# Weight ring of a transformer stack: host-ordered weights, and two expert units per transfer

## The chip, the cores and the metric

The kernel runs on one core of a Trainium2 chip. The metric is device time in microseconds (us) from start to end of one execution; lower is better.

## The reference, cut to what matters

Two blocks follow each other on 256 tokens of width 1024, all in float32. Each layer of the first block has a mixer (windowed attention in layer 0, a gated linear recurrence in layer 1) and then a mixture of experts; these two expert layers hold nearly all the weights (16 experts of 12.6 MB each, per layer). The second block has two mixers ("even" and "odd") with modulation vectors computed from `ada_w`.

```python
def expert_choice_moe(x, w_router, w_gate_up, w_down):
    aff = softmax(x @ w_router)                       # 256 x 16
    gates, idx = top_k(swapaxes(aff, 1, 2), 32)       # 32 tokens for each expert
    xs = x[bi, idx]
    g, u = split(einsum('becd,edf->becf', xs, w_gate_up), 2, axis=-1)    # 1024 x 2048 each
    out = einsum('becf,efd->becd', silu(g) * u, w_down) * gates[..., None]   # 1024 x 1024 each
    return zeros_like(x).at[bi, idx].add(out)
```

## The kernel before, in words

**The ring.** All large weights pass through a ring of eight places in the on-chip memory, `B.slot[0]` to `B.slot[7]`, of one *unit* each: 16 KB a partition, 2 MB over 128 partitions. A ninth place, the spare (number 8), lies elsewhere. An expert has four gate-up units (`gu<layer>_<expert>_<k>`) and two down units (`down<layer>_<expert>_<k>`). Other units hold the attention weights (`qkv`, `o`), the modulation weights (`ada`), the weights of the recurrence (`lru`, `rgate`, `igate`), three context units that lie between the expert units of layer 0 (`ctx_kv`, `ctx_v_lr`, `ctx_ckr`) and the weights of the even and odd mixers.

**The order.** `units()` (L240) writes out the order in which units are fetched, with the place of each and the unit that was there before. `FIRST_UNITS` (L86) fixes by hand the places of the first units of each expert layer, while modulation units still pass through. After them every unit takes the next place of the rotation (L284 to L286): eight places in layer 0, nine with the spare in layer 1. Thus a unit goes to the place that was filled longest ago.

**The fetches.** `loads()` (L511) is the program of the SyncE queue (SPq in the profile). It goes through the list in order; before each transfer it waits until the previous occupant of the place is free (L525), then issues one transfer (L536), and nothing later can pass it. The last expert of a layer fetches each down unit in four pieces (L530). A unit is set free by the matmul that reads it last: L1408 for gate-up units (after 16 matmuls of L1406), L1438 for down units (after 32 matmuls of L1436), L1475 for the last down units.

**The experts on TensorE.** `experts_tensor()` (L1340) takes the experts one by one: it waits for each gate-up unit, multiplies (L1406), hands over to ScalarE and VectorE for the activation, turns it (L1418), waits for each down unit and multiplies (L1436). Before the first expert of a layer it routes and gathers tokens (L1514, L1515), and once more between the up and the down products of the first expert. In layer 0 it also calls a side program after every second unit, which computes the context part of the even mixer from the three context units. For the last expert, two additions on TensorE (L1399) stand before each of the gate-up units 2 and 3, and `last_outs_tensor()` (L1460) multiplies the down pieces as they arrive (L1472) and adds the outcome to the tokens (L1481).

**Row lengths.** `unit_parts()` (L553) gives source and destination of each transfer. A gate-up unit reads 16 KB in one run per partition, a down unit two runs of 8 KB, most of the others eight runs of 2 KB. The two `o` units are fetched by eight transfers of 64 partitions each.

**Rounding.** For the mixers' products ScalarE (L364) writes a rounded copy of a unit into the place of `<name>_hi`, and VectorE (L380) the rest into the unit's own place. The even mixer begins with `even_narrow`, the odd mixer uses the gate blocks `ada14` and `ada15`.

Of the kernel before, what the change touches and what calls it, by code (L numbers as in the profile page):

```python
# [14 lines left out]
P = 128  # L15
D = 1024
S = 256
H = S // P
T = D // P
DEPTH = 2  # L20
# [106 lines left out]
    return out  # L127


class Signals:  # L130


# [104 lines left out]
    pass  # L237


def units():  # L240

    order, occupant, state = [], {}, {"slots": list(range(SLOTS)), "at": 0}
# [30 lines left out]
    for layer in range(DEPTH):  # L273
        experts = expert_units(layer)
        occupant[SPARE] = "lru1" if layer else None
        ring = []
        for c, i in FIRST_UNITS[layer]:
            slot = SPARE if i == SPARE else turn[i]
            if c is None:
                put(next(experts), slot)  # L280
                ring.append(slot)
            else:
                put(f"ada{layer}{c}", slot)
        state["slots"], state["at"] = ring if layer else [slot for slot in ring if slot != SPARE], 0  # L284
        for name in experts:
            put(name)  # L286
        if layer == 0:
            first = [state["slots"][(state["at"] + i) % SLOTS] for i in range(SLOTS)]
# [26 lines left out]
class Program:  # L315
# [195 lines left out]
    def loads(self):  # L511
        sig, sp, d, B = self.sig, self.sp, self.d, self.B
        sp.dma_start(B.ident, d["k_ident"]).then_inc(*sig.tell("ident_loaded", ("ident",), by=16))
        x_rows = d["x"].rearrange("o (h p) d -> p (o h) d", p=P)
        for half in range(H):
            sp.dma_start(B.x[:, half, :], x_rows[:, half, :]).then_inc(*sig.tell(f"x{half}_loaded", ("x", "input", half), by=16))
        for name, slot, before in B.units:
            if name.endswith("_hi") or name == "decay_room":
                continue
            if before is not None:  # L520
                sp.wait_ge(*sig.after("free", before))
            if name.startswith("down") and name.split("_")[1] == str(NE - 1):
                (dst, src), = self.unit_parts(name, B.slot[slot])
                for i in range(PACK):
                    sp.dma_start(dst[:, i], src[:, i]).then_inc(*sig.tell(f"last{name[-1]}{i}_loaded", ("arrived", name, i), by=16))  # L525
                continue
            if name == "qkv2":
                (dst, src), = self.unit_parts(name, B.slot[slot])
                for i in range(4):
                    pair = slice(2 * i, 2 * i + 2)  # L530
                    sp.dma_start(dst[:, pair], src[:, pair]).then_inc(*sig.tell(f"first{i}_loaded", ("arrived", name, i), by=16))
# [12 lines left out]
        sp.wait_ge(*sig.after("stored"))  # L544

    def late_rows(self):
# [3 lines left out]
        for dst, key in ((B.gain, "ln_mix_g"), (B.bias, "ln_mix_b")):  # L550
            sp.dma_start(dst, d[key][0].partition_broadcast(P)).then_inc(*sig.tell("first_rows", ("rows", "attention"), by=16))

    def unit_parts(self, name, slot):  # L553
        d = self.d
        tiles = lambda w, c0, c: w.rearrange("(p t) n -> p t n", t=T)[:, :, c0:c0 + c]
        view = lambda c: slot[:, 0:T * c].rearrange("p (t c) -> p t c", t=T)
        outs = {"lru_out": ("lru_w_out", "lru_out"), "even_out": ("even_w_out_2", "even_out"),
                "odd_out": ("odd_w_out_2", "odd_out")}
        if name[:-1] == "o":
            rows = lambda m, i: d["attn_w_o"][0][(2 * m + i) * GROUP * HD:(2 * m + i + 1) * GROUP * HD, int(name[-1]) * 512:][:, 0:512]  # L560
            return [(view(512)[64 * i:64 * i + 64, m * GROUP:(m + 1) * GROUP, :], rows(m, i).rearrange("(g d) n -> d g n", g=GROUP))
                    for m in range(2) for i in range(2)]
        if name[:-1] in outs:
            return [(view(512), d[outs[name[:-1]][0]][0].rearrange("(t p) n -> p t n", p=P)[:, :, int(name[-1]) * 512:][:, :, 0:512])]
        if name.startswith("qkv"):
            return [(view(512), tiles(d["attn_w_qkv"][0], int(name[3:]) * 512, 512))]
        if name.startswith("ada"):
            return [(view(512), tiles(d["ada_w_2"][int(name[3])], int(name[4]) * 512, 512))]
        if name.startswith("gu"):
            layer, e, k = (int(i) for i in name[2:].split("_"))  # L570
            rows = d["moe_w_gate_up"][layer][e].rearrange("(p t) n -> p t n", t=T)
            return [(slot.rearrange("p (t n) -> p t n", t=2), rows[:, 2 * k:2 * k + 2, :])]
        if name.startswith("down"):
            layer, e, k = (int(i) for i in name[4:].split("_"))
            if e == NE - 1:
                rows = d["moe_w_down"][layer][e].rearrange("(j c s) n -> c j s n", j=PACK, s=2)
                return [(slot.rearrange("p (j s n) -> p j s n", j=PACK, s=2), rows[:, :, :, k * 512:(k + 1) * 512])]
            rows = d["moe_w_down"][layer][e].rearrange("(j c s) n -> c j (s n)", j=PACK, s=2)
            return [(slot.rearrange("p (j n) -> p j n", j=2), rows[:, 2 * k:2 * k + 2, :])]
        if name.startswith("ctx"):  # L580
            _, c0, c = next(w for w in CTX_W.values() if w[0] == name)
            return [(view(c), tiles(d["even_w_in_2"][0], c0, c))]
        if name in ("lru0", "lru1", "lru2", "lru3"):
            return [(view(512), tiles(d["lru_w_in"][0], int(name[3]) * 512, 512))]
        if name in ("rgate", "igate"):
            src = d[f"lru_w_{name}"][0].rearrange("z n (c p) f -> p (z n c) f", p=P)
            return [(slot.rearrange("p (b f) -> p b f", f=LBW), src)]
        if name == "mla":
            return [(slot[:, 0:NU].rearrange("p (k n) -> p k n", k=KQ), d["mla_w_uq_2"][0].rearrange("(k p) n -> p k n", p=P)),
                    (slot[:, UNIT - MH * (MN + MV):UNIT], d["mla_w_ukv_2"][0])]  # L590
        if name.startswith("even"):
            ranges = dict(EVEN_W)[name[5:]]
            c, at, parts = sum(n for _, n in ranges), 0, []
            for c0, n in ranges:
                parts.append((view(c)[:, :, at:at + n], tiles(d["even_w_in_2"][0], c0, n)))
                at += n
            return parts
        return [(view(512), tiles(d["odd_w_in_2"][0], dict(ODD_W)[name[4:]], 512))]

    def feature_pair(self, stage, name, w, cols, h, bank, width=P):  # L600

# [2528 lines left out]
def buffers(nc, ctx):  # L3130
# [16 lines left out]
    B.slot, B.slot_r = (list(s) for s in zip(*[M.take_both(f"weight_ring{i}", UNIT) for i in range(SLOTS)]))  # L3147
# [144 lines left out]
def build(nc, dram, out):  # L3292
    with ExitStack() as ctx:
# [3 lines left out]
            Program(nc, sig, buf, dram, out, rows_dram, counting).build()  # L3297


_INS = ['x', 'attn_w_qkv', 'attn_w_o', 'attn_sink', 'lru_w_in', 'lru_conv_w', 'lru_conv_b', 'lru_w_rgate', 'lru_b_rgate',  # L3300
        'lru_w_igate', 'lru_b_igate', 'lru_lambda', 'lru_w_out', 'moe_w_router', 'moe_w_gate_up', 'moe_w_down', 'ln_mix_g',
        'ln_mix_b', 'ln_ffn_g', 'ln_ffn_b', 'c_2', 'ctx_2', 'c_ctx_2', 'ada_w_2', 'ada_b_2', 'post_ln_g_2', 'post_ln_b_2',
        'even_w_in_2', 'gla_w2_2', 'gla_b_2', 'gla_norm_g_2', 'mla_q_norm_g_2', 'mla_w_uq_2', 'mla_kv_norm_g_2', 'mla_w_ukv_2',
        'even_w_out_2', 'odd_w_in_2', 'sgu_w_2', 'sgu_b_2', 'odd_w_out_2']


# [13 lines left out]
```

## Time and profile before

| | |
|---|---|
| median of 3 runs | 1452.27 us (1452.17 to 1452.87) |
| the profiled execution | 1454.88 us, its span 1453.5 us |
| TensorE busy, mean granted clock | 1119.1 us (77%), 0.893 |
| VectorE, ScalarE, GpSimd busy | 469.0, 319.6, 91.8 us |
| SyncE's transfers (queue q1) | 492.78 MB, 83.9% of 16 engines' span |
| chain that ended last | transfers 51%, TensorE 33%, VectorE 7%, ScalarE 5% |

The span runs from the first to the last instruction; 1.4 us of the profiled execution lie around it. The layers of experts take about 118 to 590 us (layer 0) and 706 to 1165 us (layer 1). In the views of stretches the DMA column is the mean busy share of the 16 DMA engines, GB/s what they moved, and PEclk the granted clock of TensorE, 1.00 for the full 2.4 GHz and 0.50 for 1.2 GHz.

### The profile page before, as it was taken

The numbers are of one execution on the slowest core, as the hardware profiler recorded it, in microseconds if no ns is written. First come the engines' busy times: TensorE is split into PE (matmuls) and PEld (weight loads), VectorE is DVE, ScalarE is ACT, GpSimd is POOL, SyncE is SP. The second block draws the span as 40 slices with busy tenths as digits, with TensorE's granted clock in tenths as the row PEclk, the third lists the DMA queues.
The fourth block names the chain that finished last, engine by engine and source line by source line (L and its number), as shares of the span: only waits on it lengthen the run. The fifth ranks groups of instructions, "written<-read, shape, count | busy, mean of one in ns | idle before, by whom it ended". The sixth has DMA issues, their size and how long they took to land.

```text
span 1453.5 us, 19531 instructions
## 1 busy us (share of the span) xinstructions
PE 1119.1 (77%) x8573; PEld 626.9 (43%) x8573; DVE 469.0 (32%) x948; ACT 319.6 (22%) x610; POOL 91.8 (6%) x116
## 2 busy tenths in 40 slices
PE   8999756687486556999985656656655699989998
PEld 7656312253131111897631211111111288645897
DVE  4636203101210100777720100100100078565774
ACT  4512110000410000384210000000000056343450
POOL 2311100000000000050120000000000010000100
PEclk9999978799787877999998777888777999999999
DMA  9978999999999999958999999999999973204630
GB/s 306 364 273 338 417 425 426 421 424 421 423 425 426 428 425 415 359 174 339 412 389 423 427 426 426 424 425 427 426 426 424 398 287 126 107 23 173 252 116 30
DMA packets 92988, 501.29 MB, mean 345 GB/s; under 512 B 7534, under 2 KB 16196, under 8 KB 61160
## 3 DMA queue, kind: packets, MB, share of 16 engines
q1 hardware_dynamic: 87728, 492.78, 83.9%
q10 hardware_dynamic: 3112, 5.96, 1.1%
q8 instruction: 68, 1.11, 0.3%
q0 software_dynamic: 2064, 1.30, 0.3%
q14 instruction: 16, 0.13, 0.0%
HBM read 498.92 MB, written 1.10 MB: 344 GB/s over the span
## 4 chain that ended last, share of the span: by engine, by line
DMA 51%; PE 33%; DVE 7%; ACT 5%; SPq 2%; issue 1%; POOL 0%; DVEq 0%; ACTq 0%; POOLq 0%
DMA weight_ring<-in_moe_w_gate_up 31%; DMA weight_ring<-in_moe_w_down 18%; PE bank L339 5%; PE bank L1406 4%; PE bank L630 3%; PE bank L1436 3%; PE bank L340 3%; PE bank L341 3%; PE bank L342 3%; SPq L536 1%; DMA weight_ring<-in_ada_w 1%; PE bank L943 1%; PE bank L1854 1%; DVE weight_ring_rounded L380 1%; SPq L525 1%
## 5 line engine op out<-in xcount | busy, mean ns | idle before, releaser
L1406 PE MATMUL bank<-weight_ring,expert_tokens 128*32 128x512 f32 x1952 | 301.8, 753 | 169.1 <-DMA weight_ring<-in_moe_w_gate_up 164.0
L1406 PEld LDWEIGHTS bank<-weight_ring,expert_tokens 128*32 128x32 f32 x1952 | 63.2, 124 | 381.3 <-DMA weight_ring<-in_moe_w_gate_up 215.9
L1436 PE MATMUL bank<-weight_ring,actT 128*32 128x256 f32 x1760 | 139.4, 475 | 65.2 <-DMA weight_ring<-in_moe_w_down 57.3
L1644 DVE TENSOR_TENSOR act<-silu,bank 128x256 f32<-128x256 f32 x32 | 13.4, 420 | 404.8 <-ACT silu L1760 404.8
L1436 PEld LDWEIGHTS bank<-weight_ring,actT 128*32 128x32 f32 x1760 | 64.0, 132 | 131.5 <-DMA weight_ring<-in_moe_w_down 58.5
L1760 ACT ACTIVATE silu<-bank 128x256 f32<-128x256 f32 x32 | 12.3, 384 | 456.7 <-PE bank L1406 456.6
L1658 DVE COPY expert_outs<-bank 32x256 f32<-32x256 f32 x60 | 25.1, 418 | 231.9 <-PE bank L1436 231.0
L380 DVE TENSOR_TENSOR weight_ring_rounded<-weight_ring,weight_ring_rounded 128x1024 fp32r<-128x1024 f32 (+1 forms) x76 | 89.0, 1233 | 16.4 <-ACT weight_ring_rounded L364 16.2
L364 ACT CAST weight_ring_rounded<-weight_ring 128x1024 fp32r<-128x1024 f32 (+1 forms) x72 | 69.8, 1044 | 25.5 <-DMA weight_ring<-in_attn_w_qkv 11.1
L1777 ACT COPY expert_outs<-bank 32x256 f32<-32x256 f32 x60 | 21.8, 364 | 210.9 <-PE bank L1436 210.2
L494 POOL TENSOR_TENSOR norm_rstd<-norm_var,minus_half 128x1 f32<-128x1 f32 x12 | 12.1, 1008 | 848.7 <-DVE norm_var L1693 652.4
L1418 PE MATMUL bank<-ident,act 128*128 128x128 f32 x64 | 16.9, 349 | 40.9 <-DVE act L1644 40.9
L385 PE MATMUL bank<-ident 128*128 128x128 f32 x340 | 44.3, 284 | 4.7 <-DMA ident<-in_k_ident 3.7
L385 PEld LDWEIGHTS bank<-ident 128*128 128x128 f32 x340 | 41.0, 196 | 7.8 <-DMA ident<-in_k_ident 3.7
L1418 PEld LDWEIGHTS bank<-ident,act 128*128 128x128 f32 x64 | 10.1, 206 | 74.7 <-DVE act L1644 74.7
L339 PE MATMUL bank<-weight_ring,even_yT 128*128 128x512 f32 x64 | 29.3, 598 | 0.4 <-DVE even_yT L2549 0.4
L340 PE MATMUL bank<-even_h_hi_rounded,weight_ring_rounded 128*128 128x256 f32 x96 | 27.9, 290 | 1.6 <-DVE weight_ring_rounded L380 1.6
L1453 PE MATMUL bank<-expert_outs,back 128*128 128x512 f32 x48 | 25.2, 657 | 4.9 <-DVE expert_outs L1658 4.0
L339 PE MATMUL bank<-weight_ring,attention_out 128*128 128x512 f32 x64 | 28.1, 594 | 0.0
L339 PE MATMUL bank<-weight_ring,r 128*128 128x512 f32 x64 | 27.7, 593 | 0.2 <-DVE r L1959 0.2
L1854 PE MATMUL bank<-convolved,weight_ring 128*128 128x256 f32 x128 | 27.8, 379 | 0.0
L340 PE MATMUL bank<-odd_h_hi_rounded,weight_ring_rounded 128*128 128x256 f32 x96 | 27.3, 285 | 0.0
(527 smaller groups left out, 1856.5 us busy)
## 6 DMA issues: line engine op xcount, KB each, us to landing
weight_ring<-in_moe_w_gate_up SPq DMA_DIRECT2D x122, 2048.0 KB, 37.1
weight_ring<-in_moe_w_down SPq DMA_DIRECT2D x55, 2048.0 KB, 37.4
weight_ring<-in_ada_w SPq DMA_DIRECT2D x9, 2048.0 KB, 9.9
weight_spare<-in_moe_w_gate_up SPq DMA_DIRECT2D x6, 2048.0 KB, 39.8
weight_ring<-in_even_w_in SPq DMA_DIRECT2D x5, 2048.0 KB, 15.8
weight_spare<-in_moe_w_down SPq DMA_DIRECT2D x5, 2048.0 KB, 41.4
weight_ring<-in_odd_w_in SPq DMA_DIRECT2D x5, 2048.0 KB, 13.8
weight_ring<-in_moe_w_down SPq DMA_DIRECT2D x16, 512.0 KB, 29.0
```

Of the source, the lines that this page charges most:

```text
L339: return self.pe.matmul(out, sh, mh, start=start, stop=stop)
L340: self.pe.matmul(out, sl, mh, start=start, stop=False)
L341: self.pe.matmul(out, sh, ml, start=False, stop=False)
L342: return self.pe.matmul(out, sh, mh, start=False, stop=stop)
L364: a.copy(hi[:, c], raw[:, c]).then_inc(*sig.tell("weights_rounded", ("rounded", name, i)))
L380: v.tensor_tensor(lo[:, c], raw[:, c], hi[:, c], ALU.subtract).then_inc(*sig.tell("weights_split", ("weights", name, i)))
L385: self.pe.matmul(bank[:, 0:P], self.B.ident, self.B.ident, start=True, stop=True)
L630: last = pe.matmul(out, *operands, start=(parts == self.HIGH and t == 0 and first), stop=(parts == self.WEIGHTS_REST and t == T - 1), skip ...
L1406: last = pe.matmul(up[CAP * j:CAP * (j + 1), :], B.xs[:, t, e * CAP:(e + 1) * CAP], w[:, t % 2, :, j, :], start=(t == 0), stop=(t == T - 1))
L1418: last = pe.transpose(K[2][:, s * P:(s + 1) * P], B.act[i][:, s::2], B.ident)
L1436: last = pe.matmul(K[3][CAP * q:CAP * (q + 1), 0:QC], B.actT[i][:, s, j * CAP:(j + 1) * CAP], w[:, jj, s, q, :], start=(j == 0 and s == 0) ...
L1854: last = pe.matmul(self.lru_bank(job)[:, ff * S:(ff + 1) * S], w[:, z * LB + n, at:at + P], B.xc[:, 2 * n + c], start=(c == 0), stop=(c == 1))
```

## The change: what it does

The host lays all weights but the gate-up ones out as the ring holds them, so that each unit is one contiguous run per partition (`laid_out`). A down unit's run becomes 16 KB. The last down units come in runs of 4 KB. The eight places become four pairs of neighbours, and two units of an expert (gate-up 0 and 1, gate-up 2 and 3, or both down units) are fetched by one transfer of 32 KB a partition where both lie in such a pair; it waits for both previous occupants, and both units arrive with it. The rule for the places changes, and in layer 1 the spare leaves the rotation after the first units. The computation on the engines stays as it was.

```diff
+def in_pair(name):
+    if name[0:2] not in ("gu", "do"):
+        return False
+    _, e, k = name.lstrip("guodwn").split("_")
+    return int(k) % 2 == 0 and not (name.startswith("down") and int(e) == NE - 1)
@@ units()
-        state["slots"], state["at"] = ring if layer else [slot for slot in ring if slot != SPARE], 0
-        for name in experts:
-            put(name)
+        queue, names = [slot for slot in ring if slot != SPARE], list(experts)
+        while names:
+            widows = [slot for slot in queue if slot ^ 1 not in queue[0:4]]
+            pairs = [slot for slot in queue[0:4] if slot % 2 == 0 and slot + 1 in queue[0:4]]
+            if in_pair(names[0]) and pairs:
+                taken = [pairs[0], pairs[0] + 1]
+            else:
+                taken = widows[0:1] or queue[0:1]
+            for slot in taken:
+                put(names.pop(0), slot)
+                queue.remove(slot)
+                queue.append(slot)
@@ loads()
+            if i and in_pair(B.units[i - 1][0]) and slot % 2 and slot == B.units[i - 1][1] + 1:
+                continue
             if before is not None:
                 sp.wait_ge(*sig.after("free", before))
+            if in_pair(name) and slot % 2 == 0 and slot < SPARE and B.units[i + 1][1] == slot + 1:
+                other, _, other_before = B.units[i + 1]
+                if other_before is not None:
+                    sp.wait_ge(*sig.after("free", other_before))
+                src = self.pair_source(name)
+                sp.dma_start(B.slot_pair[slot // 2], src).then_inc(*sig.tell(f"slot{slot}_filled", ("arrived", name), ("arrived", other), by=16))
+                continue
@@ pair_source()
+        if name.startswith("gu"):
+            return self.d["moe_w_gate_up"][layer][e].rearrange("(p t) n -> p (t n)", t=T)[:, 2 * k * D * 2:2 * k * D * 2 + 2 * UNIT]
+        return self.d["u_down"][layer][e]
@@ unit_parts(), the general case
+        src = d[f"u_{name}"]
+        return [(slot[:, 0:src.shape[1]], src)]
```

## Rows read from the trace of the kernel before

**Rows 1.** The page, 40 equal slices of the span: DMA share and GB/s

```profile
DMA  9978999999999999958999999999999973204630
GB/s 306 364 273 338 417 425 426 421 424 421 423 425 426 428 425 415 359 174 339 412 389 423 427 426 426 424 425 427 426 426 424 398 287 126 107 23 173 252 116 30
```

**Rows 2.** Stretches inside the two expert layers: engines, PEclk, DMA share, GB/s

```profile
218.00:400.00 182.00, 122.62 (x888) 57.01 (x892) 31.89 (x81) 24.86 (x49) 1.42 (x2) 0.87 1.01 423
400.00:580.00 180.00, 119.92 (x878) 37.01 (x870) 14.71 (x33) 12.05 (x30) 0.00 (x0) 0.80 1.01 424
...
760.00:1128.00 368.00, 224.47 (x1630) 64.45 (x1634) 23.93 (x50) 20.88 (x54) 0.00 (x0) 0.79 1.01 425
```

**Rows 3.** Timeline of TensorE, layer 1: start us, us, instruction, idle before and releaser

```profile
1093.23 1.92 PE L1406 MATMUL bank<-weight_ring,expert_tokens 128*32 128x512 f32 x16 [1.50 <-DMA weight_ring<-in_moe_w_gate_up]
...
1103.16 1.93 PE L1436 MATMUL bank<-weight_ring,actT 128*32 128x256 f32 x32 [1.33 <-DMA weight_ring<-in_moe_w_down]
...
1122.73 3.27 PE L1406 MATMUL bank<-weight_ring,expert_tokens 128*32 128x512 f32 x16 [2.02 <-DMA weight_ring<-in_moe_w_gate_up]
```

**Rows 4.** Stretches around the first expert of each layer

```profile
138.00:144.00 6.00, 6.00 (x60) 1.82 (x56) 1.72 (x3) 1.25 (x1) 0.00 (x0) 1.00 0.57 208
...
728.00:734.00 6.00, 6.00 (x56) 1.99 (x49) 0.44 (x1) 0.38 (x1) 0.00 (x0) 1.00 0.80 300
```

**Rows 5.** Timeline of SyncE's queue, first expert of each layer: start us, us, transfer

```profile
139.70 0.33 SPq L536 DMA_DIRECT2D weight_ring<-in_moe_w_gate_up  x1
...
152.30 0.34 SPq L536 DMA_DIRECT2D weight_ring<-in_moe_w_gate_up  x1
...
728.43 0.33 SPq L536 DMA_DIRECT2D weight_ring<-in_moe_w_gate_up  x1
...
741.02 0.34 SPq L536 DMA_DIRECT2D weight_ring<-in_moe_w_gate_up  x1
```

**Rows 6.** Timeline of TensorE, down units of the first expert of each layer

```profile
150.30 3.66 PE L1436 MATMUL bank<-weight_ring,actT 128*32 128x256 f32 x64 [0.46 <-ACT actT L1769]
...
739.02 3.66 PE L1436 MATMUL bank<-weight_ring,actT 128*32 128x256 f32 x64 [0.46 <-ACT actT L1769]
```

**Rows 7.** Stretches with the o units, inside layer 0, and with 2 KB runs alone

```profile
28.00:32.00 4.00, 4.00 (x19) 3.23 (x18) 0.80 (x1) 1.96 (x3) 0.00 (x0) 1.00 1.07 223
...
374.00:380.00 6.00, 0.00 (x0) 0.00 (x0) 1.48 (x3) 4.40 (x6) 0.00 (x0) 0.55 1.04 437
...
1330.00:1340.00 10.00, 10.00 (x39) 4.34 (x41) 8.47 (x14) 1.80 (x4) 0.99 (x1) 1.00 1.04 385
```

**Rows 8.** Timeline of TensorE, side program and the last expert of each layer

```profile
386.24 0.70 PE L1418 MATMUL bank<-ident,act 128*128 128x128 f32 x2 [12.86 <-DVE act L1644]
...
573.90 1.92 PE L1406 MATMUL bank<-weight_ring,expert_tokens 128*32 128x512 f32 x16
...
577.82 1.92 PE L1406 MATMUL bank<-weight_ring,expert_tokens 128*32 128x512 f32 x16
...
588.65 0.64 PE L1472 MATMUL bank<-weight_ring,actT 128*32 128x128 f32 x16 [0.49 <-DMA weight_ring<-in_moe_w_down]
...
1142.51 3.62 PE L1406 MATMUL bank<-weight_ring,expert_tokens 128*32 128x512 f32 x16 [2.89 <-DMA weight_ring<-in_moe_w_gate_up]
...
1152.31 1.92 PE L1406 MATMUL bank<-weight_ring,expert_tokens 128*32 128x512 f32 x16 [0.50 <-DMA weight_ring<-in_moe_w_gate_up]
...
1164.55 0.64 PE L1472 MATMUL bank<-weight_ring,actT 128*32 128x128 f32 x16 [0.37 <-DMA weight_ring<-in_moe_w_down]
```

**Rows 9.** Timelines of ScalarE, SyncE's queue and TensorE in the even and odd stages

```profile
1169.23 1.78 ACT L364 CAST weight_ring_rounded<-weight_ring 128x896 fp32r<-128x896 f32 x2 [3.44 <-DMA weight_ring<-in_even_w_in]
1171.86 1.06 ACT L2092 ACTIVATE flat<-x_tokens 128x1024 f32<-128x1024 f32 x1 [0.84 <-DVE x_tokens L1714]
...
1327.58 3.92 SPq L536 DMA_DIRECT2D weight_ring<-in_ada_w  x1
...
1347.72 3.39 PE L943 MATMUL bank<-weight_ring,condition_columns 128*2 128x128 f32 x64 [2.94 <-DMA weight_ring<-in_ada_w]
```

More of the change, by code:

```diff
@@ L127, in constants, with laid_out @@
     return out
+def laid_out(w):
+    rows = lambda a, c0, c: a.reshape(P, T, -1)[:, :, c0:c0 + c].reshape(P, T * c)
+    out = {"u_ada": np.stack([np.stack([rows(w["ada_w_2"][layer], c * 512, 512) for c in range(NA)]) for layer in range(DEPTH)])}
+    down = w["moe_w_down"].reshape(DEPTH, NE, 2, 2, P, 2, D)
+    out["u_down"] = down[:, 0:NE - 1].transpose(0, 1, 4, 2, 3, 5, 6).reshape(DEPTH, NE - 1, P, 2 * UNIT)
+    last = w["moe_w_down"][:, NE - 1].reshape(DEPTH, PACK, P, 2, 2, 512)
+    out["u_last"] = last.transpose(0, 4, 1, 2, 3, 5).reshape(DEPTH, 2, PACK, P, UNIT // PACK)
+    for c in range(3):
+        out[f"u_qkv{c}"] = rows(w["attn_w_qkv"][0], c * 512, 512)
+    heads = w["attn_w_o"][0].reshape(2, 2, GROUP, HD, 2, 512)
+    for c in range(2):
+        out[f"u_o{c}"] = heads[:, :, :, :, c].transpose(1, 3, 0, 2, 4).reshape(P, UNIT)
+        for name, key in (("lru_out", "lru_w_out"), ("even_out", "even_w_out_2"), ("odd_out", "odd_w_out_2")):
+            out[f"u_{name}{c}"] = w[key][0].reshape(T, P, D)[:, :, c * 512:(c + 1) * 512].transpose(1, 0, 2).reshape(P, UNIT)
+    for c in range(4):
+        out[f"u_lru{c}"] = rows(w["lru_w_in"][0], c * 512, 512)
+    for name in ("rgate", "igate"):
+        out[f"u_{name}"] = w[f"lru_w_{name}"][0].reshape(-1, LBW // P, P, LBW).transpose(2, 0, 1, 3).reshape(P, UNIT)
+    out["u_mla"] = w["mla_w_uq_2"][0].reshape(KQ, P, NU // KQ).transpose(1, 0, 2).reshape(P, NU)
+    even = w["even_w_in_2"][0].reshape(P, T, -1)
+    for name, ranges in EVEN_W:
+        out[f"u_even_{name}"] = np.concatenate([even[:, :, c0:c0 + n] for c0, n in ranges], 2).reshape(P, -1)
+    for name, c0, n in CTX_W.values():
+        out[f"u_{name}"] = rows(w["even_w_in_2"][0], c0, n)
+    for name, c0 in ODD_W:
+        out[f"u_odd_{name}"] = rows(w["odd_w_in_2"][0], c0, 512)
+    return {name: np.ascontiguousarray(a) for name, a in out.items()}
 class Signals:
@@ L529, in loads @@
                 for i in range(4):
-                    pair = slice(2 * i, 2 * i + 2)
-                    sp.dma_start(dst[:, pair], src[:, pair]).then_inc(*sig.tell(f"first{i}_loaded", ("arrived", name, i), by=16))
+                    part = slice(i * UNIT // 4, (i + 1) * UNIT // 4)
+                    sp.dma_start(dst[:, part], src[:, part]).then_inc(*sig.tell(f"first{i}_loaded", ("arrived", name, i), by=16))
                 continue
@@ L551, in late_rows, with pair_source @@
             sp.dma_start(dst, d[key][0].partition_broadcast(P)).then_inc(*sig.tell("first_rows", ("rows", "attention"), by=16))
+    def pair_source(self, name):
+        layer, e, k = (int(i) for i in name.lstrip("guodwn").split("_"))
+        if name.startswith("gu"):
+            return self.d["moe_w_gate_up"][layer][e].rearrange("(p t) n -> p (t n)", t=T)[:, 2 * k * D * 2:2 * k * D * 2 + 2 * UNIT]
+        return self.d["u_down"][layer][e]
     def unit_parts(self, name, slot):
         d = self.d
[L555 to L568, printed above, removed]
         if name.startswith("gu"):
@@ L575, in unit_parts @@
             if e == NE - 1:
[L576 to L587, printed above, removed]
-        if name == "mla":
[L589 to L598, printed above, removed]
+                return [(slot.rearrange("p (j n) -> p j n", j=PACK), d["u_last"][layer][k].rearrange("j p n -> p j n"))]
+            return [(slot, d["u_down"][layer][e][:, k * UNIT:(k + 1) * UNIT])]
+        if name.startswith("ada"):
+            return [(slot, d["u_ada"][int(name[3])][int(name[4])])]
+        if name == "mla":
+            return [(slot[:, 0:NU], d["u_mla"]), (slot[:, UNIT - MH * (MN + MV):UNIT], d["mla_w_ukv_2"][0])]
+        src = d[f"u_{name}"]
+        return [(slot[:, 0:src.shape[1]], src)]
     def feature_pair(self, stage, name, w, cols, h, bank, width=P):
@@ L3146, in buffers @@
     ring = M.at
-    B.slot, B.slot_r = (list(s) for s in zip(*[M.take_both(f"weight_ring{i}", UNIT) for i in range(SLOTS)]))
+    B.slot_pair, rounded = (list(s) for s in zip(*[M.take_both(f"weight_ring{i}", 2 * UNIT) for i in range(SLOTS // 2)]))
+    B.slot, B.slot_r = ([both[i // 2][:, i % 2 * UNIT:(i % 2 + 1) * UNIT] for i in range(SLOTS)] for both in (B.slot_pair, rounded))
     room = M.at
```

16 lines of the change are left out of this document (8 added, 8 removed).

## The prediction, made before the changed kernel ran

> **What bounds the kernel now.** I read the page's slices first: in both expert layers the 16 DMA engines are fully busy at some 425 GB/s, while the stages around them move less [rows 1]. The stretches confirm it: over 182, 180 and 368 us the DMA share is 1.01 and TensorE is busy for 61 to 67% only [rows 2]. So an expert layer ends when its stream of units ends, and that is the moment from which the stream ran without a pause, plus bytes by rate. TensorE's timeline shows single arrivals, as the ends of its waits on transfers: from 1093.23 to 1103.16 two down units (9.93 us, 4.965 each), from there to 1122.73 four gate-up units (19.57 us, 4.893 each) [rows 3]. The last pause of the stream lies at the first expert: DMA share 0.57 at 138 to 144 us and 0.80 at 728 to 734 us [rows 4]. Whatever makes the transfers before this pause faster is lost in it.
>
> **1. Run lengths in the expert stream.** A down unit has 16 runs per engine, a gate-up unit 8; the difference is 4.965 - 4.893 = 0.072 us, 9 ns a run. That is my estimate of what a run costs. With 32 KB runs both have 4 per unit: a gate-up unit gains 4 x 9 = 0.037 us, a down unit 12 x 9 = 0.11 us. By the new rule of places every gate-up unit but four of layer 0 (expert 1) and eight of layer 1 (experts 0 and 1) is paired, and all down units but the last two of each layer and the first two of layer 1. In each layer 56 gate-up and 28 down units come after the pause and gain: 56 x 0.037 + 28 x 0.11 = **5.2 us a layer**. Bounds: if a 32 KB run goes no faster than two of 16 KB, only 28 x 0.072 = 2.0 us are left. If the stream reached 437 GB/s, the best 6 us inside the layers [rows 7], a unit took 4.80 us, and it were 56 x 0.09 + 28 x 0.165 = 9.7 us. I take 5.2, which extends the measured step in run length.
>
> The Trainium skill ("DMA: Bandwidth & Descriptors", section "Where 436 GB/s comes from") gives 435.2 GB/s as the ceiling of the path into the on-chip memory. By that a unit takes 4.82 us (an estimate from that page) and the gain of a layer stays below 8.2 us; no run here shows the ceiling itself, but 425 GB/s over 368 us is near it.
>
> **2. Context units.** They carry 512, 288 and 160 columns of 1024 rows, 3.9 MB. Runs of 2 KB alone move at 385 GB/s [rows 7], so 3.9 MB take 10.2 us; at 427 they take 9.2. Gain **1.0 us** in layer 0.
>
> **3. The places at the start of layer 0.** This is what I think decides. `widows` goes through the whole queue, not its first four entries, so an unpaired unit takes the first place whose neighbour is not among the oldest four: it may take a young place while old ones are free. Written out: before, `gu0_1_3` goes to place 0 after `gu0_0_0`, and is issued at 139.70, as soon as the first 16 products of expert 0 are done. Now it goes to place 6 after `down0_0_0`, free only after the first half of the down products that begin at 150.30 [rows 6]; the transfer that has this condition now is issued at 152.30 [rows 5]. SyncE's program is in order, so the pair `down0_1` and the pairs of expert 2 wait behind it although places 0 to 3 are free. The pause grows by 152.30 - 139.70 = **12.6 us**, and nothing later makes it up, since the stream never pauses again: the layer ends that much later.
>
> **4. The same in layer 1.** The pair `down1_1` takes places 0 and 1, after `gu1_0_1` and `down1_0_0`. Place 0 is free early, place 1 when the first down unit of 739.02 is done [rows 6]: 741.02, the issue that now follows it [rows 5]. Only `gu1_1_3` is issued before, at 728.43, and fills 4.9 us, to 733.3. The stream, unbroken before, stands still for 741.02 - 733.3 = **7.7 us**. Later on, four pairs in the ring leave about three in flight (29 us), enough for TensorE's longest idle time beside them, 12.86 us, with the products on both its sides [rows 8].
>
> **5. The last expert.** Its gate-up units 2 and 3 now arrive together, at the time at which 3 did. TensorE used to have finished unit 2 and one addition by then. From the start of unit 2 (573.90) to the product of the last piece (588.65), less its wait of 0.49 and about 0.3 at an earlier piece, the engine has 13.9 us of work in series. Before, 577.82 to 588.65, 10.8 us, passed after unit 3 began; in layer 1 it was 1152.31 to 1164.55, 12.2 us [rows 8]. The engine becomes what the end waits for: +3.1 and +1.7 us, and the faster last pieces bring nothing. After an idle time 16 products sometimes take 3.62 us instead of 1.92 [rows 8], the stretches average a granted clock of 0.8 [rows 2]; half such a case per layer is +0.8. Together **+3.9 and +2.5 us**; bounds 0.8 less and 1.7 more for each.
>
> **6. The even stage's first weights.** `even_narrow` now waits for `down1_15_0`, freed some 4 us before the last product. It then lands about 18 us after the last gate-up pair, and its two casts, which took 1.78 us at 1169.23, were to begin before 1171.86 [rows 9]; that instruction moves to about 21 us after the pair. Nothing, with 1 to 2 us to spare.
>
> **7. Elsewhere.** The `o` units ran at 223 GB/s beside a TensorE that was busy all of the time [rows 7]: nothing. In the recurrence TensorE, ScalarE and VectorE make the chain: nothing. At the start the rounding gets its pieces slightly earlier: -0.2. At the odd stage TensorE waits 2.94 us for the second gate block, issued last of three units at 1327.58 [rows 9]: 6.3 MB at 385 GB/s take 16.3 us, at 427 14.7: **-1.6 us**.
>
> **Sum.** Layer 0: 12.6 - 5.2 - 1.0 + 3.9 = +10.3. Layer 1: 7.7 - 5.2 + 2.5 = +5.0. Rest: -1.8. Together +13.5 us. Against the profiled execution (1454.88) that is 1468.4; against the median of the runs, 2.6 us lower, 1466.
>
> **The rivals.**
> A. *The pair is not moved in 32 KB runs*, but cut to 16 KB on the way: 3.2 us less gain a layer, **1472**. Nothing in the trace shows a run above 16 KB.
> B. *The halved number of transfers pays.* If each transfer costs something at its end, 84 pairs after the pauses save that 84 times. It decides from (13.5 + 10.4 + 2.9) / 84 = 0.32 us a pair; at 0.4 us the time is 1466 + 10.4 - 33.6 = **1443**. Against it: gate-up units follow at 4.893 us, 429 GB/s, and up to 437 only 0.09 us a unit, 0.18 a pair, are left.
> The Trainium skill (same page, "Anatomy of one DMA") gives a fixed 2.0 us for each transfer besides bytes/436e9. By that a lone unit takes 6.8 us and 84 pairs save 168 us, 1308 in all. The spacing of 4.893 us speaks against it for queued transfers, so it adds hardly anything to B's chance.
> C. *The stream pauses again*, where context units take places filled only two or three transfers before, or at the wait of 12.86 us: up to 10 us, **1476**. By my count the ring holds.
> D. *The pauses at the first experts are partly covered* by something that I don't see, or arrival in pairs costs nothing at the end, and all gains come at their upper bound: 13.5 - 9.0 - 6.4 = -1.9, **1450**.
>
> **Numbers.** Forecast 0.55, A 0.22, B 0.07, C 0.09, D 0.07. The bounds of the forecast itself: upper gains and no slow products 13.5 - 9.0 - 1.6 = +2.9, 1455; lower gains (A) and slow ones 13.5 + 6.4 + 3.4 = +23.3, 1476. The first needs all at once, so the range is 1457 to 1476. A measurement of this kernel can tell about 0.2%, 2.9 us, from no change. Faster: B and a little of D, 0.08. Same: the rest of D, 0.06. Slower: 0.86.
>
> **What would show it.** In the new timeline: `gu0_1_3` issued near 152 us, a pause of some 18 us in the stream before it and of 8 near 734 us; expert periods of 29.1 us instead of 29.5; no wait on the last down pieces, TensorE busy in their place; a wait of about 1.3 us before 1347 plus the shift. Wrong would be: a stream rate above 433 GB/s, no pause before 152 us, or a further one later.

## The result, and the profile after

The changed kernel takes 1464.49 us (median of 4 runs, 1463.13 to 1464.77) against 1452.22 us before (4 runs, 1451.75 to 1452.87): ratio 1.0081, interval 1.0068 to 1.0095, 12.3 us slower. The forecast was 1466.0, the range 1457 to 1476, and 0.86 on slower. The profiled executions are 1464.74 and 1454.88 us, their spans 1463.4 and 1453.5. The one of before lies 2.6 us above its median, so differences of spans to it come out 2 to 3 us smaller than those of medians: +9.9 here for +12.3. Where in its trace the 2.6 us lie isn't known. The ledger below is in spans, and some of its parts are too low by what is hidden there, 2.6 us at most in all.

First the page after: the slices (DMA share, GB/s) and the packets. They answer to [rows 1].

```profile
DMA  9947899999999999938979999999999974113720
GB/s 376 384 173 289 344 429 431 429 433 431 429 429 431 432 430 422 380 123 346 419 290 425 431 431 429 430 431 430 431 432 429 420 280 151 65 66 140 280 117 30
...
DMA packets 30172, 501.28 MB, mean 343 GB/s; under 512 B 5006, under 2 KB 6500, under 8 KB 12040
```

Inside, the expert layers move 429 to 433 GB/s where they moved 421 to 428, and the packets fell from 92988 to 30172. The change did what it was to do. But slices 4 and 21, the first experts of the two layers, fell from 338 to 289 and from 389 to 290 GB/s. The stretches after show both sides (columns as in [rows 2, 4]):

```profile
132.00:138.00 6.00, 5.36 (x46) 4.90 (x48) 5.45 (x12) 1.15 (x2) 0.00 (x0) 1.00 1.01 425
138.00:144.00 6.00, 6.00 (x60) 1.82 (x56) 1.80 (x3) 1.31 (x2) 0.00 (x0) 1.00 0.50 210
144.00:150.00 6.00, 5.92 (x53) 4.93 (x42) 2.08 (x4) 2.19 (x5) 0.00 (x0) 1.00 0.01 3
150.00:156.00 6.00, 5.62 (x84) 2.76 (x88) 5.58 (x11) 1.06 (x3) 0.74 (x2) 1.00 0.45 152
218.00:400.00 182.00, 126.05 (x882) 60.18 (x874) 28.59 (x73) 21.65 (x43) 1.42 (x2) 0.84 1.00 430
...
738.00:744.00 6.00, 6.00 (x57) 2.44 (x50) 0.42 (x1) 0.38 (x1) 0.00 (x0) 1.00 0.90 341
744.00:750.00 6.00, 5.54 (x67) 4.75 (x68) 3.51 (x7) 2.13 (x4) 0.00 (x0) 1.00 0.04 12
760.00:1128.00 368.00, 219.63 (x1670) 78.68 (x1674) 24.35 (x51) 21.23 (x55) 5.12 (x10) 0.80 1.00 431
```

The stream stands still from about 141 to 153 us and again from about 744 to 751 us. The first of these is 12 us long, not the 18 that the prediction named as its sign. Before, the stream stood still for some 4 us, from 136 to 140; ahead of the first stretch in [rows 4] stands there

```profile
132.00:138.00 6.00, 5.37 (x45) 4.90 (x48) 5.45 (x12) 1.21 (x3) 0.00 (x0) 1.00 0.71 293
```

Now it runs on until 141, because the two down units of expert 0 come by one transfer, which waits for both its places: SyncE issues it at 114.69, where it issued the first of the two units at 107.65. What moves the end of the layer is when the stream starts again, and that is 12.7 us later. SyncE's queue says what it stood behind: `gu0_1_3` is issued at 152.38 instead of 139.70, and in layer 1 the pair `down1_1` at 750.49, 12.65 us after the one before it, of which one unit fills 4.9 us:

```profile
152.38 0.33 SPq L592 DMA_DIRECT2D weight_ring<-in_moe_w_gate_up  x1
152.81 0.38 SPq L576 DMA_DIRECT2D weight_ring<-in_u_down  x1
...
737.84 0.33 SPq L592 DMA_DIRECT2D weight_ring<-in_moe_w_gate_up  x1
750.49 0.33 SPq L576 DMA_DIRECT2D weight_ring<-in_u_down  x1
```

TensorE's timeline in mid-layer gives the period of an expert, the distance of two equal waits: 1154.95 - 1125.81 = 29.14 us, against 29.50 before [rows 3].

```profile
1125.81 5.19 PE L1441 MATMUL bank<-weight_ring,expert_tokens 128*32 128x512 f32 x32 [4.77 <-DMA weight_ring<-in_moe_w_gate_up]
...
1154.95 5.98 PE L1441 MATMUL bank<-weight_ring,expert_tokens 128*32 128x512 f32 x32 [4.36 <-DMA weight_ring<-in_moe_w_gate_up]
```

And the last experts, which answer to [rows 8]. In layer 0 units 2 and 3 arrive together at 582.97; behind that no wait on a transfer is left, TensorE works in series to the end:

```profile
582.97 3.54 PE L1441 MATMUL bank<-weight_ring,expert_tokens 128*32 128x512 f32 x16 [2.77 <-DMA weight_ring<-in_moe_w_gate_up]
...
592.84 2.39 PE L1507 MATMUL bank<-weight_ring,actT 128*32 128x128 f32 x80
...
597.44 1.52 PE L1507 MATMUL bank<-weight_ring,actT 128*32 128x128 f32 x48
...
599.70 1.96 PE L1516 MATMUL bank<-expert_outs,back 128*128 128x512 f32 x4
...
1164.62 1.92 PE L1441 MATMUL bank<-weight_ring,expert_tokens 128*32 128x512 f32 x16 [1.77 <-DMA weight_ring<-in_moe_w_gate_up]
```

The last instruction of each layer's experts is the product with `back`: 599.70 now and 590.04 before, 1179.74 now and 1165.94 before. With these points the ledger is:

| part (us, after minus before) | forecast | measured |
|---|---|---|
| pause in layer 0 | +12.6 | +12.7 (152.38 - 139.70) |
| stream and context units, layer 0 | -6.2 | -7.5 (last gate-up unit +5.2, less 12.7) |
| last expert of layer 0 | +3.9 | +4.5 (16.7 from 582.97, was 12.2) |
| pause in layer 1 | +7.7 | +7.8 (750.49 - 742.7) |
| stream, layer 1 | -5.2 | -4.9 (with the pause +2.9) |
| last expert of layer 1 | +2.5 | +1.5 (15.1 from 1164.62, was 13.6) |
| between the layers | 0 | -0.3 |
| odd stage | -1.6 | -3.9 |
| start, even stage | -0.2 | 0 |
| sum | +13.5 | +9.9 (spans +9.9) |

### The profile page after: what moved, and what is told of

Its sections match the earlier page's. It is cut to its first block, busy times and chain, and to the rows that moved or that the text cites. A ratio compares the mean times of both kernels' runs of the same rounds, so it can differ in the third digit from the quotient of the medians.

```text
span 1463.4 us, 19515 instructions
## 1 busy us (share of the span) xinstructions
PE 1121.4 (77%) x8573; PEld 654.4 (45%) x8573; DVE 468.2 (32%) x948; ACT 319.7 (22%) x610; POOL 87.9 (6%) x116
## 4 chain that ended last, share of the span: by engine, by line
DMA 46%; PE 38%; DVE 8%; ACT 5%; issue 1%; POOL 0%; SPq 0%; DVEq 0%; ACTq 0%; POOLq 0%
DMA weight_ring<-in_moe_w_gate_up 33%; DMA weight_ring<-in_u_down 12%; PE bank L1441 8%; PE bank L386 5%; PE bank L1471 3%; PE bank L665 3%; PE bank L387 3%; PE bank L389 3%; PE bank L388 3%; PE bank L1889 1%; DVE weight_ring_rounded L427 1%; PE bank L978 1%; DMA weight_ring<-in_u_qkv 1%; PE bank L432 1%; PE bank L2704 1%
## 5 line engine op out<-in xcount | busy, mean ns | idle before, releaser
L1441 PE MATMUL bank<-weight_ring,expert_tokens 128*32 128x512 f32 x2016 | 314.2, 780 | 182.3 <-DMA weight_ring<-in_moe_w_gate_up 177.3
L1441 PEld LDWEIGHTS bank<-weight_ring,expert_tokens 128*32 128x32 f32 x2016 | 78.1, 138 | 401.1 <-issue 281.4
L1471 PE MATMUL bank<-weight_ring,actT 128*32 128x256 f32 x1920 | 156.6, 498 | 75.1 <-DMA weight_ring<-in_u_down 72.8
L1471 PEld LDWEIGHTS bank<-weight_ring,actT 128*32 128x32 f32 x1920 | 85.8, 142 | 137.6 <-issue 118.5
L1795 ACT ACTIVATE silu<-bank 128x256 f32<-128x256 f32 x32 | 12.3, 384 | 466.3 <-PE bank L1441 466.3
L427 DVE TENSOR_TENSOR weight_ring_rounded<-weight_ring,weight_ring_rounded 128x1024 fp32r<-128x1024 f32 (+1 forms) x76 | 89.0, 1234 | 13.8 <-ACT weight_ring_rounded L411 13.7
L541 POOL TENSOR_TENSOR norm_rstd<-norm_var,minus_half 128x1 f32<-128x1 f32 x12 | 12.1, 1008 | 848.9 <-DVE norm_var L1728 651.6
## 6 DMA issues: line engine op xcount, KB each, us to landing
weight_spare<-in_u_ada SPq DMA_DIRECT2D x3, 2048.0 KB, 12.3
```

Of the source, the lines that this page charges most:

```text
L427: v.tensor_tensor(lo[:, c], raw[:, c], hi[:, c], ALU.subtract).then_inc(*sig.tell("weights_split", ("weights", name, i)))
L1441: last = pe.matmul(up[CAP * j:CAP * (j + 1), :], B.xs[:, t, e * CAP:(e + 1) * CAP], w[:, t % 2, :, j, :], start=(t == 0), stop=(t == T - 1))
L1471: last = pe.matmul(K[3][CAP * q:CAP * (q + 1), 0:QC], B.actT[i][:, s, j * CAP:(j + 1) * CAP], w[:, jj, s, q, :], start=(j == 0 and s == 0) ...
```

## The experiments

Ten runs, in three groups that each shared their runs of the kernel before (1452.44, 1452.23 and 1452.11 us). Edits are against the changed kernel where nothing else is said. My theory was the ledger: a faster stream (9 ns a run and engine), overpaid by two pauses and by TensorE's series at the end. The rival was that pairing as such, one transfer of 32 KB for two, costs or gains something of its own.

### e1_widows: the rule for unpaired units

```diff
-            widows = [slot for slot in queue if slot ^ 1 not in queue[0:4]]
+            widows = [slot for slot in queue[0:4] if slot ^ 1 not in queue[0:4]]
```

> The changed kernel, but an unpaired unit takes its place among the four oldest only, so that gu0_1_3 takes place 0 after gu0_0_0. Theory (the pause at the first expert of layer 0 is carried whole to the end, and comes from this choice of a place): gu0_1_3 issued near 139.7 us instead of 152.4, no stretch without transfers between 144 and 150 us, and 12.4 us less, about 1452, level with the kernel before. Layer 1 keeps its pause of 7.8 us. Rival (a ring of four pairs is too shallow whatever place comes first): little changes, 1460 or more.

1453.05 us (10 runs, 1451.56 to 1454.46), ratio to before 0.9996, interval 0.9987 to 1.0006: 11.4 us faster than the changed kernel (12.4 expected), by one expression. The stretches of this run, the last for the pause in layer 1, which was left as it is:

```profile
138.00:144.00 6.00, 6.00 (x62) 1.69 (x52) 1.37 (x3) 0.90 (x1) 0.00 (x0) 1.00 0.96 385
144.00:150.00 6.00, 5.54 (x53) 4.97 (x49) 2.51 (x5) 2.52 (x5) 0.00 (x0) 1.00 1.07 434
...
734.00:742.00 8.00, 7.54 (x105) 3.88 (x107) 5.45 (x12) 1.69 (x4) 2.25 (x4) 1.00 0.53 189
```

The pause of layer 0 is gone, and `gu0_1_3` is issued at 139.36, 13.0 us earlier than in the changed kernel (0.4 of it because the program ran that much earlier there already: the transfer in front stands at 128.51 instead of 128.93). The layer's end comes at 586.75 instead of 599.70, 12.95 us earlier. The pause is carried in full.

### e2_tail: gate-up units 2 and 3 of the last expert in two transfers

```diff
+def alone(name):
+    return name in ("gu0_15_2", "gu1_15_2")
@@ loads()
-            if i and in_pair(B.units[i - 1][0]) and slot % 2 and slot == B.units[i - 1][1] + 1:
+            if i and in_pair(B.units[i - 1][0]) and slot % 2 and slot == B.units[i - 1][1] + 1 and not alone(B.units[i - 1][0]):
@@ and the same in the branch that issues a pair
```

> The changed kernel, but gate-up units 2 and 3 of the last expert of each layer are fetched by two transfers, to the same places. Theory (the joint arrival makes TensorE late at the end of a layer, measured as 4.5 us in layer 0 and 1.5 in layer 1): waits on the last down pieces come back, and 6 us less, about 1458. Rival (the end of a layer was longer because of the slow clock or of the later issue of the last down units): 1463 to 1465.

1459.41 us (1458.16 to 1460.66), 1.0040, interval 1.0027 to 1.0053: 5.1 us less than the changed kernel. Layer 0 ends at 595.52, 4.2 us earlier, layer 1 at 1172.98, 6.8 earlier, so 2.6 of its own. That is more than the 1.5 of the ledger: the wait of 1.77 for the last pair is gone, and the products of units 0 and 1 took 5.05 us where they took 5.98. But the waits on the last pieces did not come back. TensorE in layer 0:

```profile
573.02 5.34 PE L1446 MATMUL bank<-weight_ring,expert_tokens 128*32 128x512 f32 x32 [4.37 <-DMA weight_ring<-in_moe_w_gate_up]
...
588.54 2.40 PE L1512 MATMUL bank<-weight_ring,actT 128*32 128x128 f32 x80
...
593.14 1.63 PE L1512 MATMUL bank<-weight_ring,actT 128*32 128x128 f32 x48
...
595.52 1.97 PE L1521 MATMUL bank<-expert_outs,back 128*128 128x512 f32 x4
```

From 573.02, the joint arrival of units 0 and 1, there is no further wait on a transfer: the series is merely set going one pair earlier. So the experiment shows that the arrival of units 2 and 3 together cost time, but its theory of what would set the end instead was wrong. e9_last_single returns to that.

### e4_pause: the pause alone, in the kernel before

```diff
             if before is not None:
                 sp.wait_ge(*sig.after("free", before))
+            if name == "gu0_1_3":
+                sp.wait_ge(*sig.after("free", "down0_0_0"))
```

> The kernel before with one added wait: SyncE's queue also waits for down0_0_0 to be free before it fetches gu0_1_3. Theory (a pause of the stream ahead of the saturated stretch is never made up): gu0_1_3 issued near 152.3 instead of 139.7, 12.6 us more, about 1465. Rival (the deep ring makes up for most of it, and the loss of the changed kernel has another cause): less than 5 us more.

1467.09 us (1464.57 to 1467.81), 1.0090, interval 1.0073 to 1.0106: +14.6 by the medians, +13.0 by the spans. `gu0_1_3` was issued at 153.17, 13.5 us later than in the profile of before (0.8 of it because the whole program ran that much later there already: the transfer in front of it stands at 129.65 instead of 128.85), and the end of layer 0 moved by 13.6, from 590.04 to 603.60. One wait of one transfer costs its length, although in the kernel before that unit was fetched well ahead of its use: its products are the last 16 of 48 that run there from 155.50 to 160.83.

### e3_halves: each pair by two transfers of 16 KB

Places, waits and the moment of arrival stay.

```diff
-                sp.dma_start(B.slot_pair[slot // 2], src).then_inc(*sig.tell(f"slot{slot}_filled", ("arrived", name), ("arrived", other), by=16))
+                dst = B.slot_pair[slot // 2]
+                sp.dma_start(dst[:, 0:UNIT], src[:, 0:UNIT]).then_inc(*sig.tell(f"slot{slot}_filled", by=16))
+                sp.dma_start(dst[:, UNIT:], src[:, UNIT:]).then_inc(*sig.tell(f"slot{slot}_filled", ("arrived", name), ("arrived", other), by=16))
```

> The changed kernel with each pair fetched by two transfers of 16 KB a partition, one behind the other, with the same places and the same waits; both units count as arrived with the second. Theory (the gain in the stream is one of run length, 9 ns a run and engine: 84 pairs x 8 more runs x 9 ns = 6.0 us after the pauses): expert periods of 29.35 us instead of 29.14, about 1470.5. Rival (32 KB runs are worth nothing beyond 16 KB): 1464.5. Rival (each transfer costs something at its end, 0.3 us or more): 1490 or more.

1470.61 us (1470.05 to 1470.73), 1.0116, interval 1.0101 to 1.0131: +6.1 on the changed kernel. The period of an expert is 1140.48 - 1111.11 = 29.37 us:

```profile
1111.11 5.34 PE L1443 MATMUL bank<-weight_ring,expert_tokens 128*32 128x512 f32 x32 [4.59 <-DMA weight_ring<-in_moe_w_gate_up]
...
1140.48 6.05 PE L1443 MATMUL bank<-weight_ring,expert_tokens 128*32 128x512 f32 x32 [4.37 <-DMA weight_ring<-in_moe_w_gate_up]
```

This run changes two things at once, though: the length of the runs and the number of transfers. The next one parts them.

### e8_short_runs: down pairs by one transfer, in runs of 8 KB

```diff
@@ pair_source(), and the destination seen as four runs
-        return self.d["u_down"][layer][e]
+        return self.d["moe_w_down"][layer][e].rearrange("(j c s) n -> c j (s n)", j=PACK, s=2)
```

> The changed kernel, but each pair of down units is read by its one transfer from the original array, in four runs of 8 KB a partition instead of one of 32 KB. Places, waits and number of transfers stay. Theory (run length): 28 pairs after the pauses x 24 more runs x 9 ns = 6.0 us more, about 1470.5, expert periods of 29.35 us. Rival (the number of transfers sets the gain): 1464.5, periods of 29.14.

1471.26 us (1468.87 to 1473.67), 1.0122, interval 1.0101 to 1.0144: +6.8 by the medians. The runs spread over 4.8 us, and the spans are only 4.1 apart, so the period says more here. The number of transfers is that of the changed kernel, the runs of an expert are those of e3_halves (two gate-up pairs of 8 runs per engine and a down pair of 32, 48 together, against 24), and so is the period, 1139.01 - 1109.65 = 29.36 us. The gain of the change hangs on the runs, not on the transfers.

```profile
1080.29 6.24 PE L1442 MATMUL bank<-weight_ring,expert_tokens 128*32 128x512 f32 x32 [4.64 <-DMA weight_ring<-in_moe_w_gate_up]
...
1090.30 6.36 PE L1472 MATMUL bank<-weight_ring,actT 128*32 128x256 f32 x64 [2.29 <-DMA weight_ring<-in_moe_w_down]
...
1109.65 5.22 PE L1442 MATMUL bank<-weight_ring,expert_tokens 128*32 128x512 f32 x32 [4.72 <-DMA weight_ring<-in_moe_w_gate_up]
...
1139.01 5.90 PE L1442 MATMUL bank<-weight_ring,expert_tokens 128*32 128x512 f32 x32 [4.29 <-DMA weight_ring<-in_moe_w_gate_up]
```

### e5_layout: the host's layout alone

No pairs, and the rotation of nine places of the kernel before:

```diff
-        queue, names = [slot for slot in ring if slot != SPARE], list(experts)
-        while names:
...
+        state["slots"], state["at"] = ring if layer else [slot for slot in ring if slot != SPARE], 0
+        for name in experts:
+            put(name)
```

> Only the host's layout: the weights laid out by the host, but the places of the kernel before and one transfer for each unit. Theory (run length at 9 ns, and no lost time at the ends of the expert layers): 28 down units a layer with 8 runs less (4.0 us in both), context units 1.0, last pieces 1.2, odd stage 3.9 as in the changed kernel, start 0.3: about 10.4 less than before, 1442. Rival (the layout's gains lie in stages that wait for something else): 1448 or more.

1444.36 us (1443.73 to 1445.69), 0.9940, interval 0.9920 to 0.9961: faster than both kernels. The medians are 7.9 us apart, 2.5 less than expected. The span (1442.4) is 11.1 us shorter than before, and where that comes from can be read from the same points as above: the end of layer 0 at 586.08 (-4.0), of layer 1 at 1158.74 (-7.2), the odd stage 1343.78 instead of 1354.85 (-11.1, so -3.9 again). The two measures differ by 3.2 us, because the profile of before lies 2.6 above its median and this one 0.6 below; the parts are together too large by that, and the traces don't say which of them. Six transfers and 48 runs an expert give 29.36 us once more:

```profile
1106.70 3.29 PE L1437 MATMUL bank<-weight_ring,expert_tokens 128*32 128x512 f32 x16 [2.88 <-DMA weight_ring<-in_moe_w_gate_up]
...
1136.06 1.92 PE L1437 MATMUL bank<-weight_ring,expert_tokens 128*32 128x512 f32 x16 [1.34 <-DMA weight_ring<-in_moe_w_gate_up]
```

### e6_all and e7_single: the corrections together, with and without pairs

e6_all has the edits of e1_widows and e2_tail, and in layer 1 the two down units of expert 1 go singly to the oldest places:

```diff
-            if in_pair(names[0]) and pairs:
+            if names[0] in ("down1_1_0", "down1_1_1"):
+                taken = queue[0:1]
+            elif in_pair(names[0]) and pairs:
```

> The changed kernel with three corrections: unpaired units take their place among the four oldest, down1_1_0 and down1_1_1 take the oldest place each and are fetched singly, and gate-up units 2 and 3 of the last expert are fetched singly. Theory: the pauses of 12.7 and 7.8 us and the 6 us at the ends of the layers go, the gains in the stream stay: 1437 to 1440, the fastest so far. Rival (places of four pairs cost further time in flight): 1446 or more.

1440.16 us (1440.12 to 1440.89), 0.9910, interval 0.9893 to 0.9926: 24.3 us less than the changed kernel and 12.1 less than the kernel before. Neither pause is left. The stretches of layer 0, which stood at 210 and 3 GB/s in the changed kernel, and those of layer 1 around its pause, of which the first stood at 189 in e1_widows:

```profile
138.00:144.00 6.00, 6.00 (x64) 1.72 (x56) 1.45 (x3) 0.97 (x1) 0.00 (x0) 1.00 0.99 390
144.00:150.00 6.00, 5.57 (x50) 4.92 (x42) 2.44 (x5) 2.52 (x5) 0.00 (x0) 1.00 1.02 415
...
734.00:742.00 8.00, 8.00 (x108) 3.46 (x112) 4.05 (x10) 0.73 (x2) 2.25 (x4) 1.00 1.01 426
742.00:750.00 8.00, 6.58 (x94) 3.07 (x90) 0.42 (x1) 0.76 (x2) 2.54 (x5) 1.00 1.05 444
```

e7_single keeps all places of e6_all and fetches every unit by itself (`alone` returns True).

> The kernel with the three corrections, and every expert unit fetched singly, with 16 KB runs, to the same places. Theory (run length): 168 units x 4 more runs x 9 ns = 6.0 us more than the corrected kernel with pairs, 1443 to 1446, and within 2 us of the layout alone. Rival (a pair also costs by its later arrival, unseen in the middle of a layer): level with the corrected kernel with pairs.

1444.06 us (1444.02 to 1444.45), 0.9936, interval 0.9919 to 0.9952: 3.9 us slower than e6_all, where 6 were expected, and level with e5_layout. So pairs at good places are worth 3.9 us. Of the missing 2 us, 1.3 lie at the end of layer 0, which e6_all reaches only 1.1 us before e7_single (584.97 and 586.08) though its stream is 2.4 us ahead (unit 1 arrives at 562.27 and 564.67). TensorE in e6_all:

```profile
562.27 5.74 PE L1448 MATMUL bank<-weight_ring,expert_tokens 128*32 128x512 f32 x32 [4.66 <-DMA weight_ring<-in_moe_w_gate_up]
...
569.85 1.92 PE L1448 MATMUL bank<-weight_ring,expert_tokens 128*32 128x512 f32 x16
...
584.97 1.96 PE L1523 MATMUL bank<-expert_outs,back 128*128 128x512 f32 x4
```

After the joint arrival at 562.27 nothing waits for a transfer any more: 22.7 us of TensorE's work in series, as in e2_tail (22.5 from 573.02).

### e9_last_single, with e6_again: the last expert's gate-up units one by one

```diff
-    return name in ("gu0_15_2", "gu1_15_2")
+    return name[4:7] == "15_"
```

> As e6_all, and gate-up units 0 and 1 of the last expert of each layer come by two transfers as well, so that all four arrive one by one. Theory: in e6_all no wait on a transfer is left in layer 0 behind the joint arrival of units 0 and 1 at 562.27 (the next products stand at 569.85 and 573.61 without a wait), so TensorE's work in series from there, 22.70 us to 584.97, sets the end, which is why the tail experiment gained less than the arrivals alone would give, and e6_all only 1.1 us in layer 0 over its version with single transfers. With unit 0 some 4.8 us earlier its products are done beforehand: unit 1's begin at about 562.3 and the chain behind is that of e7_single from its unit 1, 564.67 to 586.08 = 21.4 us: end of layer 0 at 583.7, 1.3 us earlier. In layer 1 e7_single has 22.8 us from unit 1 (1136.12) to 1158.92, as e6_all has from the pair: nothing. Time 1438.9 (1438 to 1440). Rival: the last down pieces set the end in both, then nothing changes: 1440.2.

> e6_all once more on the same chip as e9_last_single, for a comparison to 0.1%: both theories expect 1440.2 (1439.8 to 1441).

e9_last_single 1439.28 us (1438.61 to 1440.47), 0.9911, interval 0.9898 to 0.9925; e6_again 1441.18 us (1439.69 to 1441.88), 0.9920, interval 0.9906 to 0.9933. The times alone don't part the two, the intervals overlap; the traces do. TensorE in e9_last_single:

```profile
563.03 1.92 PE L1449 MATMUL bank<-weight_ring,expert_tokens 128*32 128x512 f32 x16 [2.18 <-DMA weight_ring<-in_moe_w_gate_up]
567.92 1.92 PE L1449 MATMUL bank<-weight_ring,expert_tokens 128*32 128x512 f32 x16 [1.05 <-DMA weight_ring<-in_moe_w_gate_up]
572.83 1.92 PE L1449 MATMUL bank<-weight_ring,expert_tokens 128*32 128x512 f32 x16 [1.07 <-DMA weight_ring<-in_moe_w_gate_up]
...
584.72 1.96 PE L1524 MATMUL bank<-expert_outs,back 128*128 128x512 f32 x4
```

In e6_again the pair arrives at the same moment, and the end comes 1.6 us later:

```profile
563.02 6.36 PE L1448 MATMUL bank<-weight_ring,expert_tokens 128*32 128x512 f32 x32 [6.07 <-DMA weight_ring<-in_moe_w_gate_up]
...
586.35 1.96 PE L1523 MATMUL bank<-expert_outs,back 128*128 128x512 f32 x4
```

23.3 us of series against 21.7 with waits: the explanation of the two shortfalls holds, and a wait on a transfer again stands before each of these products. The size is less certain. The first e6_all took 22.7 us from the same arrival, because its 32 products took 5.74 us instead of 6.36, so the gain is 1.0 to 1.6 us for the 1.3 expected.

## Why the prediction was right, point by point

**The pauses (steps 3 and 4)** were the core and came out to 0.1 us each (12.7 for 12.6, 7.8 for 7.7), at the places and behind the units named. Only the standstill of 18 us, named as a sign, was wrong, because the later issue of the first down pair was overlooked; it changed nothing in the sum. e1_widows takes the first pause away and gets back 12.95 us at the end of its layer; e4_pause puts it alone into the kernel before and moves the end by 13.6. Nothing covered them, so rival D had no ground.

**The stream (step 1).** The estimate of 9 ns a run and engine was drawn from one row and held for all compositions: 64 runs an expert 29.50 us, 48 runs 29.36 to 29.37 (four kernels), 24 runs 29.14. From 64 to 24 that is 0.36 / 40 = 9.0 ns, from 48 to 24 0.225 / 24 = 9.4, from 64 to 48 0.135 / 16 = 8.4; with periods read to 0.01 us the three can't be told apart. The down pair alone says the same: 10.01 us with 32 runs (1080.29 to 1090.30 in e8_short_runs), 9.80 with 8 (1106.30 to 1116.10 in the changed kernel), 0.21 for 24 runs. So there was neither a cut to 16 KB (rival A, whose time e3_halves shows, 1470.6 for the 1472 said) nor a gain by the number of transfers (rival B): an expert with 48 runs takes 29.36 us by six transfers and by three. The Trainium skill (DMA: Bandwidth & Descriptors, section Anatomy of one DMA) gives a fixed 2.0 us for a transfer issued by GpSimd. The prediction took it for any transfer; the ones here are issued by SyncE, and these runs show no such cost for transfers that stand queued. Nor did the stream pause again (rival C): its DMA share is 1.00 at 218 to 400, 400 to 570 and 760 to 1128 us. In layer 0 the term was 1.3 us too small (7.5 for 6.2); what of that is the context units' and what lies before the pause wasn't taken apart.

**The last expert (step 5)** cost 4.5 and 1.5 us for 3.9 and 2.5. The mechanism was right: in both layers the last pieces wait for nothing. The 0.8 us for slow products was a mean of two cases that both occurred: the first 16 products took 3.54 us in layer 0, at a granted clock of 0.52, and 1.92 in layer 1, at 1.00. That the two layers fell one to each side is luck. The fix by e2_tail showed where my picture was too short. I had let the series begin at unit 2; with unit 2 alone it begins at units 0 and 1, 22.5 us before the end.

**The even stage (step 6)** came as said, +13.8 like the end of layer 1, but there was less to spare than the 1 to 2 us. ScalarE after:

```profile
1183.78 1.78 ACT L411 CAST weight_ring_rounded<-weight_ring 128x896 fp32r<-128x896 f32 x2 [4.19 <-DMA weight_ring<-in_u_even_narrow]
1185.66 1.06 ACT L2127 ACTIVATE flat<-x_tokens 128x1024 f32<-128x1024 f32 x1
```

The casts end at 1185.56, 0.1 us before the instruction that they could have delayed.

**The odd stage (step 7)** is the term that was mis-sized: -3.9 for -1.6. TensorE after:

```profile
1358.47 1.93 PE L978 MATMUL bank<-weight_ring,condition_columns 128*2 128x128 f32 x64
1362.34 1.16 PE L2093 MATMUL bank<-ident,flat 128*128 128x128 f32 x8 [0.40 <-DVE flat L2108]
1364.81 4.09 PE L665 MATMUL bank<-odd_h_hi_rounded,weight_ring_rounded 128*128 128x256 f32 x32 [0.65 <-ACT odd_h_hi_rounded L2151]
```

I had worked out the wait from 385 and 427 GB/s and left 1.3 us of the 2.94; it is gone whole, and with it a second cost that I left out: the 64 products behind it took 3.39 us after the idle time [rows 9], at a granted clock of 0.55, and take 1.93 without it, at 1.00. 2.94 + 1.46 less a new wait of 0.40 for VectorE is 4.0. e5_layout, without any pair, has the same three rows in the same durations and the same -3.9, so it comes from the layout. In e4_pause, with the layout of before, the wait (2.21) and the slow products (3.52) are still there. Measured against that trace instead of the one of before, the stage is 3.2 us shorter, so 0.6 of the 3.9 may be chance.

**The rate.** The Trainium skill (DMA: Bandwidth & Descriptors, section Where 436 GB/s comes from) gives 435.2 GB/s as the ceiling; 431 over 368 us stayed under it, as the forecast had it. Single stretches of 6 to 8 us read above it (444 in e6_all, with a DMA share of 1.05). No share can be above 1, so the view of short stretches is that inexact, and they decide nothing; the bound of 437 in step 1 came from such a stretch [rows 7].

In all, the spans came out 3.6 us under the sum: 0.6 in layer 0, 0.9 between the ends of the two layers, 2.1 behind them, nearly all of it the odd stage. By the medians the change is +12.3, 1.2 under the sum of 13.5, and that is why the time came out within 1.5 us of the 1466.

## What to carry to other kernels

Where a stage is bound by its stream of transfers, look first at what a new order of buffers makes the in-order queue wait for: one transfer put to a young place cost 12.7 us, more than all longer runs of that layer brought (7.5). Joining two arrivals is good in mid-stream, where the consumer has slack, and bad in front of an end, where it turns overlap into a series: join everywhere but in the last expert, and check again after each repair, since the series then starts one arrival earlier. A faster layout can be had without the joining: here the layout alone brought 7.9 us, pairs at good places 3.9 more.

## What the runs showed of the hardware that I had not expected

The cost of a run is nearly the same from 8 to 32 KB: 8.4 to 9.4 ns a run and engine, with nothing per transfer that the period of an expert shows (29.36 us by six or by three). Periods of equal composition agree to 0.01 or 0.02 us between kernels, so the period of one profile is enough to weigh a layout, where the times spread by 1 us and more.

Products that follow an idle time can take 3.3 to 3.6 us for what takes 1.92 to 1.93 otherwise, and at times something between. The length of the idle time doesn't tell which; in the kernel before and in e7_single:

```profile
567.90 3.64 PE L1406 MATMUL bank<-weight_ring,expert_tokens 128*32 128x512 f32 x16 [1.17 <-DMA weight_ring<-in_moe_w_gate_up]
...
1072.57 1.93 PE L1448 MATMUL bank<-weight_ring,expert_tokens 128*32 128x512 f32 x16 [3.04 <-DMA weight_ring<-in_moe_w_gate_up]
```

The granted clock does. It is 0.50 over the first of these, from 567.90 to 571.50, and had been 0.50 since 561 us, through two idle times and the 16 products between them; from 573.90, after products without a gap, it is 1.00 again. In the second it is 1.00, as it was in the idle time before. Half the clock, 1.2 GHz for 2.4, is about twice the time. A wait that goes away can thus bring more than its length, as the odd stage shows.
